# A conv mixer by seven products in place of eight, scaled probabilities, exchanged rotary halves, and experts with gate and up apart

## The reference

```python
h = h + short_conv_mixer(rmsnorm(h), conv_w_in, conv_w, conv_w_out)     # layer 0
h = h + hier_moe(rmsnorm(h), ...)
h = h + mla_mixer(rmsnorm(h), w_dq, cq_g, w_uq, w_o, k_nope, k_rope, v, cos, sin)  # layer 1
h = h + hier_moe(rmsnorm(h), ...)

def short_conv_mixer(hn, w_in, conv_w, w_out):
    b, c, u = jnp.split(hn @ w_in, 3, axis=-1)      # hn: 1040 x 1024, w_in: 1024 x 3072
    z = causal_depthwise_conv(c * u, conv_w)        # 3 taps
    return (b * z) @ w_out
```

## Time and profile before

| | us |
|---|---|
| median of the runs (3064.04 to 3065.76) | 3064.82 |
| the profiled execution | 3065.33 |
| its span, first to last instruction | 3063.6 |
| conv mixer, PE from 701.1 | 338 |
| heads, from 1877.3 | 447 |
| first expert stage, PE from 1230.7 | 512 |
| second expert stage, PE from 2489.9 | 514 |

### The profile page before, as it was taken

One profiled execution on the slowest core, in us unless ns is written; L12 is line 12 of the kernel. 1 busy time (PEld: TensorE's weight loads), 2 busy tenths in 40 slices (PEclk: granted clock), 3 DMA queues, 4 the chain that ended last, 5 costly groups with the idle time before them and its releaser, 6 DMA issues. The chain is left out here.

```text
span 3063.6 us, 36378 instructions
## 1 busy us (share of the span) xinstructions
PE 2695.4 (88%) x14806; PEld 1462.0 (48%) x14806; DVE 930.1 (30%) x2308; ACT 549.3 (18%) x1386; POOL 176.9 (6%) x255
## 2 busy tenths in 40 slices
PE   8999999998999898978787699999999978878872
PEld 3445579645666555323233265656665533323330
DVE  2414656452110145211011153434443432111114
ACT  0212455210000011111011131321221111111111
POOL 1000000000000000111111000000000011111110
PEclk9999999999999998999899899999999979988996
DMA  3111010221112045799999760020002469999995
GB/s 106 35 34 49 1 44 5 72 83 55 42 41 101 23 190 206 310 420 420 420 419 418 288 244 1 18 97 1 1 1 97 179 247 419 420 420 419 416 401 214
DMA packets 104937, 564.54 MB, mean 184 GB/s; under 512 B 20896, under 2 KB 21056, under 8 KB 52400
## 3 DMA queue, kind: packets, MB, share of 16 engines
q1 hardware_dynamic: 78432, 500.83, 40.8%
q0 software_dynamic: 21440, 43.51, 3.8%
q10 hardware_dynamic: 4896, 17.83, 1.4%
HBM read 529.84 MB, written 65.01 MB: 194 GB/s over the span
## 5 line engine op out<-in xcount | busy, mean ns | idle before, releaser
L1996 PE MATMUL ex__h_ps<-all__arena,ex__xT 128*64 128x512 f32 x1696 | 523.9, 670 | 172.8 <-DMA all__arena<-in_w_up 112.8
L1996 PEld LDWEIGHTS ex__h_ps<-all__arena,ex__xT 128*64 128x64 f32 x1696 | 169.3, 154 | 474.5 <-issue 470.1
L1505 PE MATMUL cm__acc<-all__arena,cw__w 128*128 128x352 f32 (+1 forms) x1152 | 338.0, 457 | 2.3 <-PEq L81 2.3
L287 PE MATMUL fr__acc<-X__xT,fr__w 128*128 128x512 f32 x640 | 280.8, 599 | 8.0 <-DMA X__xT<-in_xT 7.8
L1505 PEld LDWEIGHTS cm__acc<-all__arena,cw__w 128*128 128x128 f32 x1152 | 220.1, 191 | 120.0 <-issue 4.3
L1293 PE MATMUL pb__acc<-b__w,all__arena 128*128 128x512 f32 x544 | 244.8, 605 | 12.5 <-POOL pb__eps L1247 12.5
L2024 DVE TENSOR_TENSOR ex__hs<-ex__sg,ex__h_ps 128x256 f32<-128x256 f32 x64 | 27.0, 422 | 680.9 <-ACT ex__sg L2021 680.7
L287 PEld LDWEIGHTS fr__acc<-X__xT,fr__w 128*128 128x128 f32 x640 | 121.7, 192 | 164.7 <-issue 155.1
L1996 PE MATMUL ex__h_ps<-mo__wx,ex__xT 128*64 128x512 f32 x352 | 181.1, 674 | 0.0
L1293 PEld LDWEIGHTS pb__acc<-b__w,all__arena 128*128 128x128 f32 x544 | 102.7, 193 | 132.1 <-issue 118.4
L2010 PE MATMUL ex__y_ps<-b__w,ex__hT 128*64 128x512 f32 x672 | 153.5, 599 | 1.4 <-ACT ex__hT L2027 1.4
(11 more groups left out here) (417 smaller groups left out, 3506.5 us busy)
## 6 DMA issues: line engine op xcount, KB each, us to landing
all__arena<-in_w_gate SPq DMA_DIRECT2D x106, 1024.0 KB, 22.0
all__arena<-in_w_up SPq DMA_DIRECT2D x106, 1024.0 KB, 26.4
b__w<-in_w_down SPq DMA_DIRECT2D x84, 1024.0 KB, 20.7
all__arena<-in_w_down SPq DMA_DIRECT2D x22, 1024.0 KB, 16.9
mo__wx<-in_w_down SPq DMA_DIRECT2D x22, 1024.0 KB, 24.6
mo__wx<-in_w_gate SPq DMA_DIRECT2D x22, 1024.0 KB
mo__wx<-in_w_up SPq DMA_DIRECT2D x22, 1024.0 KB
all__arena<-s_ys SPq DMA_DIRECT2D x16, 1024.0 KB, 9.0
```

The lines of the kernel that those rows point to most:

```text
L287: last = mm(acc[:, b, c], wbuf[:, b, k], xT[:, k, 512 * c:512 * c + 512], start=(k == 0), stop=(k == KT - 1))
L1505: last = nc.tensor.matmul(acc[:, u % 2, s, 0:cols], w[:, j % 2, s, k], hnT[:, k, at:at + cols], start=(k == 0), stop=(k == KT - 1))
L1996: last = nc.tensor.matmul(h_ps[half, b].rearrange("p (a b) -> p a b", a=2), xT[:, b, k, half], slots[n][:, :, k], start=(k == 0), stop=(k ...
```

## The change

**Conv mixer.** Strassen's scheme in Winograd's form, with 7 products in place of 8 for a 2 x 2 split. A unit is one of the b, c, u sets for two tiles of output columns (`m` = 0, 1), so there are 4 x 3 = 12 units, in the order c, u, b. The contraction is split into two halves of 4 slices and the 1040 rows into two halves of 520, each of these worked in two cuts of 260 columns (`c` = 0, 1). DVE makes sums of weight tiles (512 columns each) and, once per cut, sums of rows (4 x 260 columns each); PE makes the products M1, M5, M6, M7, M2, M4, M3 of 4 slices each into 8 banks in turn; ACT copies M1 out; DVE adds the products up with seven sums.

```diff
+CONV_UNITS = [(i, s) for i in range(KT // 2) for s in CONV_SETS]     # CONV_SETS = (1, 2, 0)
+TH = T // 2
+TC = TH // 2
+HK = KT // 2
...
-                for j in range(1, KT):
-                    if j >= 2:
-
-                        sp.wait_ge(done, NC * (j - 1))
-                    sp.dma_start(w[:, j % 2], D["conv_w_in_t"][j]).then_inc(w_loaded[j % 2], 16)
+                for n in range(3, NU):
+
+                    sp.wait_ge(product, 14 * (n - 2))
+                    conv_weight(sp, D, w, w_loaded, n)
...
+                def mul(u, x, weight, moving, c):
+                    for k in range(HK):
+                        last = nc.tensor.matmul(bank(u, x), weight(k), moving(k, c), start=(k == 0), stop=(k == HK - 1))
+                    last.then_inc(product, 1)
...
+                        if u >= 2:
+                            pe.wait_ge(summed, 7 * (u - 2) + C12)
+                        mul(u, M1, a11, b11, c)
+                        pe.wait_ge(s_made, 4 * n + 1)
+                        pe.wait_ge(t_made, 4 * c + 1)
+                        if u:
+                            pe.wait_ge(e1_out, u)
+                        mul(u, M5, s1, t1, c)
...
+                            pe.wait_ge(summed, 7 * (u - 1) + V5)
+                        mul(u, M6, s2, t2, c)
...
+                        mul(u, M7, s3, t3, c)
+                        mul(u, M2, a12, b21, c)
+                        if u:
+                            pe.wait_ge(summed, 7 * (u - 1) + C11)
+                        pe.wait_ge(t_made, 4 * c + 4)
+                        mul(u, M4, a22, t4n, c)
+                        if u:
+                            pe.wait_ge(summed, 7 * (u - 1) + C21)
+                        pe.wait_ge(s_made, 4 * n + 4)
+                        mul(u, M3, s4, b22, c)
...
+                def first_sums(n, i, s, c):
...
+                    dve.wait_ge(product, 7 * u + M6 + 1)
+                    add(u, U2, u2, e1[:, u % 2], bank(u, M6))
+                    dve.wait_ge(product, 7 * u + M7 + 1)
+                    add(u, W, c21, u2, bank(u, M7))
+                    add(u, C22, c22, c21, bank(u, M5))
+                    add(u, V5, c12, u2, bank(u, M5))
+
+                def last_sums(n, i, s, c):
...
+                    dve.wait_ge(product, 7 * u + M2 + 1)
+                    add(u, C11, c11, e1[:, u % 2], bank(u, M2))
+                    dve.wait_ge(product, 7 * u + M4 + 1)
+                    add(u, C21, c21, c21, bank(u, M4))
+                    dve.wait_ge(product, 7 * u + M3 + 1)
+                    add(u, C12, c12, c12, bank(u, M3))
...
+                for i in range(KT // 2):
...
+                    first_sums(nc_, i, 1, 0)
+                    if i == 0:
+                        row_sums(1, 1, 2, 3, 4)
+                    last_sums(nc_, i, 1, 0)
+                    weight_sums(nu, 1, 2, 3, 4)
+                    first_sums(nc_, i, 1, 1)
+                    last_sums(nc_, i, 1, 1)
...
+                    gated(nu, i)
...
+                    tap(i, 0, 0)
+
+                    first_sums(nb, i, 0, 0)
+                    tap(i, 0, 1)
+                    tap(i, 0, 2)
+                    last_sums(nb, i, 0, 0)
```

```diff
+                def exchange(j):
+
+                    sp.wait_ge(raw_out, 2 * (j + 1))
+                    for at in range(0, P, ROPE):
+                        for a, b in ((at, at + ROPE // 2), (at + ROPE // 2, at)):
+                            sp.dma_start(rot[a:a + ROPE // 2], raw[b:b + ROPE // 2]).then_inc(exchanged, 16)
+
+                exchange(0)
                 for j in range(2, NPAIR):
...
                     pre.pair(sp, j)
+                    exchange(j - 1)
+                exchange(NPAIR - 1)
                 next_loads(sp)
...
-                    pe.wait_ge(exped, 2 * u + h + 1)
+                    pe.wait_ge(normed, 2 * u + h + 1)
...
-                    pe.wait_ge(diag_done, 2 * u + h + 1)
-                    mm(o_ps[:, h, P:2 * P], ones[:], dg[:, h, u % 2], start=True, stop=True).then_inc(mixed, 1)
+                    last.then_inc(mixed, 1)
...
-                        V.tensor_scalar(dg[:, h, p], ident[:], rl[:, h, p:p + 1], None, ALU.mult).then_inc(diag_done, 1)
+                        V.tensor_scalar(pr[:, h, p, 0:keys], pr[:, h, p, 0:keys], rl[:, h, p:p + 1], None,
+                                        ALU.mult).then_inc(normed, 1)
...
-                        v(V.tensor_copy(ob[:, h], o_ps[:, h, P:2 * P]))
-                        tt(oT[:, 2 * j + h, P * i:P * i + P], o_ps[:, h, 0:P], ob[:, h], ALU.mult).then_inc(oout, 1)
+                        V.tensor_copy(oT[:, 2 * j + h, P * i:P * i + P], o_ps[:, h, 0:P]).then_inc(oout, 1)
...
-                    diagonals(j, 0)
+                    norms(j, 0)
                     for n in range(1, NB):
                         biggest(j, n)
+                        norms(j, n)
                         output(j, n - 1)
-                        diagonals(j, n)
```

```diff
+                    sp.wait_ge(m["g_done"], p - RING + 1)
+                    for n in range(2):
+                        gate_in(sp, gu_slots[r][n], p + n * PAIRS_M, g_loaded[r])
                     sp.wait_ge(m["h_done"], p - RING + 1)
                     for n in range(2):
-                        gate_up(sp, gu_slots[r][n], p + n * PAIRS_M, gu_loaded[r])
+                        up_in(sp, gu_slots[r][n], p + n * PAIRS_M, u_loaded[r])
...
-                    pe.wait_ge(gu_loaded[p % RING], 64 * (p // RING + 1))
-                    gate_up_products(p % 2, gu_slots[p % RING]).then_inc(m["h_done"], 1)
+                    pe.wait_ge(g_loaded[p % RING], 32 * (p // RING + 1))
+                    gate_products(p % 2, gu_slots[p % RING]).then_inc(m["g_done"], 1)
+                    if p >= 1:
+                        last_product(p - 1)
+                    pe.wait_ge(u_loaded[p % RING], 32 * (p // RING + 1))
+                    up_products(p % 2, gu_slots[p % RING]).then_inc(m["h_done"], 1)
                     if p + 1 < PAIRS_M:
                         turn(p + 1)
-                    if p >= 1:
-                        last_product(p - 1)
```

More of the change, by code:

```diff
@@ L1509, in _ @@
             @block.scalar
             def _(act):
-                for j in range(KT):
-                    if j >= 2:
-                        act.wait_ge(conv_done, j - 1)
-                    for n, (at, cols) in enumerate(CUTS):
-                        u = NC * j + n
-                        act.wait_ge(done, u + 1)
-                        if u >= 2:
-                            act.wait_ge(z_made, u - 1)
-                        nc.scalar.copy(bT[:, j % 2, at:at + cols], acc[:, u % 2, 0, 0:cols])
-                        nc.scalar.copy(cT[:, u % 2, 0:cols], acc[:, u % 2, 1, 0:cols]).then_inc(copied, 1)
+                for u in range(2 * NU):
+                    act.wait_ge(product, 7 * u + M1 + 1)
+                    if u >= 2:
+                        act.wait_ge(summed, 7 * (u - 2) + C11)
+                    nc.scalar.copy(e1[:, u % 2], bank(u, M1)).then_inc(e1_out, 1)
@@ new lines, in dest, with add @@
+                def dest(i, s, m, cols):
+                    return z[:, i % 2, m, 2 + cols.start:2 + cols.stop] if s == 1 else ub[:, m, cols]
+                def add(u, result, out, a, b, op=ALU.add):
+                    V.tensor_tensor(out, a, b, op).then_inc(summed, 1)
+                    dve.wait_ge(summed, 7 * u + result)
+                def first_sums(n, i, s, c):
+                    u = 2 * n + c
+                    c11, c12, c21, c22 = (dest(i, s, m, cols) for m in range(2) for cols in (low(c), high(c)))
+                    dve.wait_ge(e1_out, u + 1)
+                    dve.wait_ge(product, 7 * u + M6 + 1)
[4 more added lines that the diff above has]
+                    add(u, V5, c12, u2, bank(u, M5))
@@ new lines, in gated, with tap @@
+                def gated(n, i):
+                    v(V.tensor_tensor(z[:, i % 2, :, 2:2 + T], z[:, i % 2, :, 2:2 + T], ub[:], ALU.mult))
+                def tap(i, m, s):
+                    j = 2 * i + m
+                    if s == 0:
+                        v(V.tensor_scalar(zT[:, j, 0:T], z[:, i % 2, m, 0:T], taps[:, j, 0:1], None, ALU.mult))
+                    else:
+                        v(V.scalar_tensor_tensor(out=zT[:, j, 0:T], in0=z[:, i % 2, m, s:s + T], scalar=taps[:, j, s:s + 1],
+                                                 in1=zT[:, j, 0:T], op0=ALU.mult, op1=ALU.add))
@@ L2778, in moe @@
         back_and_route(nc, D, layer, tokens, src, out.h_in, h_out, keep, out, x_loaded, early, late)
-        experts(nc, D, layer, tokens, keep, spill, gate, gu_slots, d_slots, xe, gu_loaded, d_loaded, x_loaded, next_loads)
+        experts(nc, D, layer, tokens, keep, spill, gate, gu_slots, d_slots, xe, g_loaded, u_loaded, d_loaded, x_loaded, next_loads)
 def program_parts(nc, D, arena, gate):
```

268 lines of the change are left out of this document (176 added, 92 removed).

## The result

The changed kernel takes 2973.44 us in the median of 4 runs (2971.66 to 2974.91), the kernel before 3065.29 (3064.04 to 3065.96, 4 runs): a ratio of 0.9701, with an interval of 0.9684 to 0.9717. The forecast was 2966, with a range of 2950 to 2998. The profiled execution took 2971.66 us with a span of 2969.9; before it was 3065.33 and 3063.6.

A forecast was written before the change was run, and what follows sets the result against it. PE was taken to bound the conv mixer and heads, DMA the experts. From the profiled 3065.3 us, -44.1 (mixer), -36.9 (heads) and -18.2 (experts) gave 2966.1, forecast 2966 us, range 2950 to 2998.

The forecast's parts named there:

- Conv mixer, -44.1: Conv mixer stage: fewer PE columns -41.5 us, start wait +0.5, shorter end -3.1; bounds -20 to -45.3.
- 4 us of slack per sum: Conv mixer: every DVE sum is ready 4 us or more before PE needs it, so only 0.5 us is lost.
- Rivals C: Conv mixer: PE waits for DVE's sums, 1 us per half, giving 2990 us; chance 7%.
- rival D: Conv mixer: weight loads don't run beside 260-column passes, 0.407 us a pass, about 3217 us in all; chance 3%.
- Heads, exchange, -20.6: Heads: the second product for the exchanged rotary queries goes, 20.6 us less; the SBUF copies replacing it cost 0.
- Heads, diagonal, -17.3: Heads: the product of ones with the diagonal goes 64 times at 0.27 us, 17.3 less (13.6 to 20.5).
- Heads, scaling 0 and waits +1: Heads: DVE's scaling of probabilities is covered by the next unit's scores, 0 us; PE's waits for transposed tiles add 1.
- Rival B: Heads: transposes wait for DVE's scaling in every unit, up to 38 us: 3004, half of that 2985; chance 10%.
- Experts, start, 4.6 a layer: Expert stages' start: pair 0's down product ends 4.6 us earlier, DMA then has backlog and the whole stream shifts.
- Experts, end, 4.5 a layer: Expert stages' end: gate lands 5.0 us before up, so the last product starts at L + 7.3, 4.5 us earlier.
- Rival A: Expert stages keep time: gate and up land together (2975 us), or pair 0 is no earlier either (2984); chance 14%.
- 26 us for the experts: Expert stages: the largest saving in the bounds (0 to -26) given for the two layers' -18.2 us.

The follow-up runs named there:

- use_order: The changed kernel with expert weight loads issued as gate, down of the pair before, up, in place of gate, up, down: 2965.12 us, ratio 0.9668 to the kernel before.

## Why the prediction was right, and where not

**Conv mixer, -44.1: measured -43.6.** 1344 passes in 297.2 us (forecast 296.5 plus 0.5 for the start), so 260 columns keep the column rate; a sum with a PSUM operand takes 0.424 us (0.43). The tail is 2.9 us (3.0). The claim of 4 us of slack per sum was not measured as such; the cover holds for double the work of every sum. Rivals C and D are out: the trace has no wait of PE for DVE in the mixer, and a pass takes 0.221 us with a weight load of 0.19 beside it. That measurement is against the sentence of the Trainium skill quoted with rival D ("TensorE: Matmul & The Clock Gate", The mechanism).

**Heads, exchange, -20.6: measured -20.2.** The four copies land 2.4 us after issue (median of 16); the bound of 6.2 was far above. DVE's operation on the exchanged rows starts 0.14 us behind the DVE copy ahead of it (second pair, 1945.94), without a wait for them.

**Heads, diagonal, -17.3: measured -14.9. This is the step that was mis-sized.** The prediction took 0.27 a piece "because part of the 0.32 looks like the change from the 16-row tile, which stays", and so split the difference. All of it stays: 0.32 less the 0.1 that now falls on the next scores is 0.22, two passes at 0.112, and 64 x 0.22 is 14.3. The lower bound of 13.6 was the nearer row. The same mistake hid a larger thing: the rate of 0.127 us a pass, read from 2.29 us for 18 passes that end in the 16-row tile, is 18 x 0.112 = 2.0 and nearly 0.3 for that tile.

**Heads, scaling 0 and waits +1: measured 0 and 0.** PE waits for ACT and DVE as before, to 0.3 us. Rival B is out: no transposes wait for a scaling.

**Experts, start, 4.6 a layer.** The first gate reload goes out 6.2 us after PE's first gate pass (5.6 forecast, 9.3 before), the first down reload 18.6 (18.3 forecast, 22.9 before). Most of the 0.6 us that the first reload is late goes with the clock: gate and up of pair 0 took 9.6 us where they took 9.2 before, with a granted clock of 0.58 in the first 8 us (1188 to 1196) where it was 0.62 (1231.7 to 1239.7). The last up weights land 3.7 us earlier after the first transposes (1679.9 less 1187.0, against 1727.3 less 1230.7), 0.9 short. The prediction moved the down reload and did not ask what stands behind it in SP's list, the next gate loads: DMA had no backlog yet, as "from there DMA has backlog" wants it, but a hole of 1.4 us (the estimate above), which `use_order` filled.

**Experts, end, 4.5 a layer.** The last product starts 6.9 us after the last up weights land (7.3 forecast, 11.8 before), and gate lands 5.4 us ahead of up (5.0 forecast). So to the last product both layers have their 9: -8.6 and -9.8. In the first layer 2.3 of it comes back behind the last product, since the next stage's loads are not through and the last scatter lands later. The prediction counted to the last product and took the rest as fixed. Rival A is out: with a semaphore each, the last gate weights landed 5.4 us ahead of the last up weights. But the medians of the earlier trace rows that the prediction set against it could not show this, as said above; the term stood on less than it seemed.

**The rest.** Block one took 1.2 us more, back and route 1.3 less and 1.4 more, though none of their instructions was changed. The second back and route lies between 163.4 and 165.7 us over all kernels here, with no part of the change that goes with it; what moves it stays open. The sum was 5.5 us of span too good (99.2 for 93.7): 1.3 of it in these untouched stages, 0.5 in the mixer, 1.9 in the heads, 1.8 in the experts. Some luck is in this: the 1 us for waits that did not come hides as much of the diagonal's 2.4, and an end of the first expert stage 0.4 better than forecast hides part of its start. Each part that was changed still fell short, so the total rests on no large error that cancels another. By the medians the saving is 91.9 us and the forecast 7.4 off; most of the rest is the changed kernel's median lying 1.8 above its profiled execution. The range is less well founded: its lower end takes 26 us for the experts, which no step works out (the 26 of the text is a cost), and by the rivals' own chances at most 14% lie outside, not about 15%.

## What to carry to other kernels

Price a removed instruction by a neighbour that stands between equals: a pass behind one with fewer rows also carries a cost of that one, and this cost stays when the pass goes. Where a product has a short contraction (few rows) next to full ones, fill it up with zeros and measure. In a stage bound by DMA, write the loads in the order in which the slots come free, and look at what stands behind each waiting load; the gain then ends where the next stage's loads end.

## What the runs showed of the hardware that was not expected

A tile of 16 rows (two passes) among tiles of 128 costs 0.33 to 0.37 us beyond its passes, in four steps between starts of 0.200 to 0.213 us where full passes go at 0.112, while the weight loads of both take 183 and 192 ns in the median. The steps are of the size of a load, as if it did not run beside the pass before it; this reading is argued and not shown. The Trainium skill ("TensorE: Matmul & The Clock Gate", Step-by-step: what each phase is for) says that the row count doesn't matter for the time of a load; for the load by itself the rows agree, for the sequence they don't: 23.6 us of the heads' 413 went when all passes of the mix had 128 rows.

DVE took every sum of the mixer twice, 231 us of work in place of 161, for 1.1 us of time.
